# Row order in the two split parts of the normalised rows, and a gather that reads its stationary operand with a stride

## What is computed

```python
h = layer_norm(DN_ALPHA * h + mix @ w_out[l], ln1_g[l], ln1_b[l])
ff = hier_moe(h, w_grp[l], b_grp[l], w_exp[l], b_exp[l], w_gate[l], w_up[l], w_down[l])
ple = (p[l] @ w_ple[l]) * jax.nn.sigmoid(h @ w_ple_gate[l])
h = layer_norm(DN_ALPHA * h + ff + ple, ln2_g[l], ln2_b[l])
# in hier_moe:
hg = jnp.einsum('td,edf->tef', xt, w_gate)
hu = jnp.einsum('td,edf->tef', xt, w_up)
h = jax.nn.silu(hg) * hu * combine[:, :, None].astype(hg.dtype)
return jnp.einsum('tef,efd->td', h, w_down).reshape(B, S, D)
```

## Time and profile before

| | |
|---|---|
| median of 3 runs | 1613.43 us (1612.69 to 1613.9) |
| the profiled execution, its own time | 1613.67 us |
| its span in the profile | 1611.9 us |
| TensorE matmul busy | 1501.9 us (93%) |
| TensorE weight loads busy | 1000.9 us (62%) |
| VectorE, ScalarE, GpSimd busy | 659.7, 494.5, 67.7 us |
| mean granted TensorE clock | 0.984 of full speed |
| DMA | 394.83 MB, 245 GB/s over the span |

### The profile page before, as it was taken

One profiled execution on the slowest core, in us unless ns is written; L12 is line 12 of the kernel. 1 busy time (PEld: TensorE's weight loads), 2 busy tenths in 40 slices (PEclk: granted clock), 3 DMA queues, 4 the chain that ended last, 5 costly groups with the idle time before them and its releaser, 6 DMA issues.

```text
span 1611.9 us, 16579 instructions
## 1 busy us (share of the span) xinstructions
PE 1501.9 (93%) x6640; PEld 1000.9 (62%) x6640; DVE 659.7 (41%) x896; ACT 494.5 (31%) x662; POOL 67.7 (4%) x69
## 2 busy tenths in 40 slices
PE   8999999999999999999999989979988998898872
PEld 6887888887778888888888856423423532342221
DVE  5546665466566554545456544000111021011116
ACT  4444444455544444444444323100200100020011
POOL 0000000046000000000000020000000000000001
PEclk9999999999999999999999998999999999999996
DMA  8654555554434556555659451697999799879991
GB/s 291 190 175 157 181 163 200 163 174 140 153 122 144 182 190 201 183 199 191 195 185 348 165 188 52 278 419 298 373 422 411 299 376 422 350 316 422 422 401 57
DMA packets 130250, 394.83 MB, mean 245 GB/s; under 512 B 11264, under 2 KB 13952, under 8 KB 105600
## 3 DMA queue, kind: packets, MB, share of 16 engines
q1 hardware_dynamic: 121600, 384.45, 64.6%
q10 hardware_dynamic: 8576, 9.36, 1.7%
HBM read 391.69 MB, written 2.10 MB: 244 GB/s over the span
## 4 chain that ended last, share of the span: by engine, by line
PE 80%; DMA 17%; DVE 1%; ACTq 1%; issue 1%; ACT 0%; SPq 0%; POOL 0%; DVEq 0%
PE bank L449 18%; PE bank L450 18%; PE bank L454 17%; DMA moe_ring<-in_w_gate_dram 9%; PE bank L805 7%; PE bank L849 7%; DMA moe_ring<-in_w_down_dram 4%; PE bank L880 4%; DMA moe_ring<-in_w_ple_gate_dram 3%; PE bank L829 2%; PE bank L744 1%; PE bank L779 1%; PE bank L476 1%; PE bank L607 1%; PE bank L629 1%; DMA w_ring<-in_w_in_dram 1%
## 5 line engine op out<-in xcount | busy, mean ns | idle before, releaser
L1411 DVE TENSOR_TENSOR w_lo<-w_ring,w_hi 128x1024 fp32r<-128x1024 f32 (+1 forms) x312 | 381.9, 1226 | 307.4 <-ACT w_hi L1017 306.5
L1017 ACT ACTIVATE w_hi<-w_ring 128x1024 fp32r<-128x1024 f32 (+1 forms) x312 | 327.2, 1050 | 317.0 <-PE bank L454 309.3
L449 PE MATMUL bank<-w_hi,xT_hi 128*128 128x512 f32 (+1 forms) x864 | 347.3, 402 | 2.3 <-ACT w_hi L1017 2.3
L450 PE MATMUL bank<-w_hi,xT_lo 128*128 128x512 f32 (+1 forms) x864 | 335.9, 389 | 0.0
L849 PE MATMUL bank<-moe_ring,xg 128*64 128x512 f32 x1024 | 231.0, 597 | 35.4 <-DMA moe_ring<-in_w_gate_dram 18.2
L454 PE MATMUL bank<-w_lo,xT_hi 128*128 128x512 f32 (+1 forms) x864 | 229.4, 387 | 0.0
L449 PEld LDWEIGHTS bank<-w_hi,xT_hi 128*128 128x128 f32 x864 | 162.7, 188 | 38.8 <-issue 7.1
L849 PEld LDWEIGHTS bank<-moe_ring,xg 128*64 128x64 f32 x1024 | 69.9, 137 | 183.3 <-issue 130.3
L450 PEld LDWEIGHTS bank<-w_hi,xT_lo 128*128 128x128 f32 x864 | 163.0, 189 | 32.6 <-issue 1.9
L454 PEld LDWEIGHTS bank<-w_lo,xT_hi 128*128 128x128 f32 x864 | 161.8, 188 | 33.4
L880 PE MATMUL bank<-moe_ring,moe_hiddenT 128*64 128x512 f32 x448 | 103.3, 606 | 17.2 <-DMA moe_ring<-in_w_down_dram 17.2
(11 more groups left out here) (265 smaller groups left out, 1372.4 us busy)
## 6 DMA issues: line engine op xcount, KB each, us to landing
w_ring<-in_w_in_dram SPq DMA_DIRECT2D x104, 1024.0 KB, 5.0
moe_ring<-in_w_gate_dram SPq DMA_DIRECT2D x32, 2048.0 KB, 15.0
moe_ring<-in_w_up_dram SPq DMA_DIRECT2D x32, 2048.0 KB, 15.6
moe_ring<-in_w_down_dram SPq DMA_DIRECT2D x32, 2048.0 KB, 16.1
w_ring<-in_w_proj_a_dram SPq DMA_DIRECT2D x16, 1024.0 KB, 5.0
w_ring<-in_w_proj_m_dram SPq DMA_DIRECT2D x16, 1024.0 KB, 5.1
w_ring<-in_w_out_dram SPq DMA_DIRECT2D x16, 1024.0 KB, 5.1
moe_ring<-in_w_ple_gate_dram SPq DMA_DIRECT2D x8, 2048.0 KB, 16.8
```

Of the source, the lines that this page charges most:

```text
L449: mm(b, lh(k, m), WH[:, s, kk, 0:width], start=start and kk == 0, stop=False)
L450: mm(b, ll(k, m), WH[:, s, kk, 0:width], start=False, stop=False)
L1017: fn(WH[:, h % 4, :, 0:width], W32[:, h // 2, 2 * (h % 2):2 * (h % 2) + 2, 0:width], ACT.Copy).then_inc(hi_ready, 1)
L1411: v.tensor_tensor(WL[:, h % 4, :, 0:width], W32[:, h // 2, 2 * (h % 2):2 * (h % 2) + 2, 0:width], WH[:, h % 4, :, 0:width].bitcast(F32), A ...
```

## The change

`h1_hi` and `h1_lo` are laid out as [half, 2048] in the order of the rows, as `res` is. ScalarE's copy and VectorE's subtraction are now plain, over 2048 adjacent words. `gather_pair` picks column 16 q + t for q = 0 to 127 out of a row of 2048, so each weight load of the gather reads 128 words that stand 16 words apart, where it read 128 adjacent words. Shapes, types, counts, waits and the order of instructions on every engine are the same. The same function serves the overflow branch, which runs when an expert has more than 64 tokens; the trace has none of its instructions.

```diff
-        h1h = at("h1_hi", [NT, KT, P], Z2, F32R)
-        h1l = at("h1_lo", [NT, KT, P], Z2 + 16384, F32R)
+        h1h = at("h1_hi", [NT, D], Z2, F32R)
+        h1l = at("h1_lo", [NT, D], Z2 + 16384, F32R)
...
                     for part, src in enumerate((h1h, h1l)):
                         for a in range(NT):
-                            last = mm(b[:, kk * TOK:kk * TOK + TOK], src[:, a, 2 * i + kk, :], selg[:, a, :],
+                            last = mm(b[:, kk * TOK:kk * TOK + TOK], src[:, a, 2 * i + kk:D:KT], selg[:, a, :],
                                       start=part == 0 and a == 0, stop=part == 1 and a == 1)
...
             for a in range(NT):
-                fn(h1h[:, a, :, :].rearrange("p t q -> p q t"), RES[:, a, :].rearrange("p (q t) -> p q t", t=KT),
-                   ACT.Copy).then_inc(h1_hi, 1)
+                fn(h1h[:, a, :], RES[:, a, :], ACT.Copy).then_inc(h1_hi, 1)
...
                 dv.wait_ge(h1_hi, a + 1)
-                v.tensor_tensor(h1l[:, a, :, :].rearrange("p t q -> p q t"), RES[:, a, :].rearrange("p (q t) -> p q t", t=KT),
-                                h1h[:, a, :, :].rearrange("p t q -> p q t").bitcast(F32), ALU.subtract).then_inc(h1_lo, 1)
+                v.tensor_tensor(h1l[:, a, :], RES[:, a, :], h1h[:, a, :].bitcast(F32), ALU.subtract).then_inc(h1_lo, 1)
```

## The result

The change makes the kernel slower: 1639.9 us in the median (1638.81 to 1640.6, four runs) against 1613.66 us for the kernel before in the same comparison, a ratio of 1.0162 with a 95% interval of 1.0145 to 1.018. That is 26.2 us. It lies above the range given, and within half a microsecond of the time of the rival that I had given a chance of 0.16. The profiled execution spans 1638.4 us.

A forecast was written before the change was run, and what follows sets the result against it. TensorE's four gathers were taken to bound the end, with DMA engines idle beside them. The sum was 1613.67 + 0 to 1.8 - 0 - 0, forecast 1613.5 us against the median; 8-in-10 range 1611.5 to 1628.5.

The forecast's parts named there:

- What bounds the kernel: All four gathers lie on the path to the end; DMA engines idle beside them, so longer gathers count in full.
- the price: One nanosecond more per matmul of the four gathers, 256 matmuls in all, costs 0.256 us at the end.
- The pace inside a gather: A matmul starts every 120 ns, set by 256 streamed columns; adjacent loads leave the loader 8 to 10 ns slack.
- Part 1: Gather's strided weight loads: they come every 113 ns, under 120, so cost 0, at most 1.8 us.
- The upper bound of 7 ns: Gather's weight loads: if loads limit it, each gets 196 - 189 = 7 ns longer, 1.8 us in all.
- The rule against it: SBUF reads by the gather's loads: each new 16-byte line pays a penalty, so fp32 strides are free only to 4 words.
- Parts 2 and 3: ScalarE's copies save 3.6 us, VectorE's subtractions about 3.1 us; both disappear into waits ended by TensorE, worth 0.
- The halved rate: Gather's strided loads go from 112 to 224 ns each, 26.6 us more, time 1640; chance 0.16.
- Its further fear: In the gathers, less streaming could drop TensorE's clock to the 1.2 GHz level and take the time above 1640.

The follow-up runs named there:

- the split order: The change, strided loads included, with all four gathers split between ring slots: ratio 1.0119 against the kernel before, 1.0143 against the same order with adjacent loads.
- the ladder: Kernel before, the gather's eight pairs loading with strides of 1, 2, 3, 4, 5, 8, 12 and 16 words; one run, 1635.57 us.
- the half-strided kernel: Kernel before with h1_lo in row order and loaded with a stride, h1_hi still adjacent, so half of 256 loads strided: 1628.67 us, ratio 1.0096.

## Why the prediction was wrong, point by point

- **What bounds the kernel.** Right. The gathers were on the path, the price of 0.256 us per nanosecond and matmul held: 103 ns more give 26.4 us, and 26.2 were measured. Half of the loads gave about half. The reason given, that the DMA engines start later by what the gather grows, fits every trace: 93.5 to 94.2 us from the load behind gather 1 or 2 to the next gated product. A load issued sooner was tried at gather 0 alone, where it gained; under the split order 2 us of the longer gather 0 were hidden, so the price holds for the order of work it was read from.
- **The pace inside a gather.** Right. Adjacent words left slack, and the ladder's stride 2 still hides in it.
- **Part 1, the step that failed.** I wrote that I take the cadence of 113 ns of the strided transposes "as the deciding row", and that "an ordinary load is at the slower rate already". Both took a transpose for an ordinary load. The runs show that the plain 4-byte load with a stride of 16 has a cadence of its own, 217 to 225 ns, in fp32r with 64 and 256 columns and in f32 with 128, where I had put 113. That is the term of the sum that failed: 0 to 7 ns per matmul were forecast, and 103 came. The rows had a warning that I noted and explained away: an adjacent transpose lasts 139 ns and an adjacent ordinary load 189, for the same 128 words. If the two take different ways with adjacent words, the pace of one with a stride says nothing about the other. The upper bound of 7 ns drawn from that comparison was worth nothing.
- **The rule against it.** The rule of the 16-byte line (the Trainium skill, "SBUF — State Buffer", Door 1: The DMA port swizzle) was to be trusted more than the nearest row of another kind of operation, though its free stride of 4 words is not what was measured here.
- **Parts 2 and 3.** Right in size and in worth: plain copies of 1.90 and 2.29 us, all of the gain in longer waits, and the ratio of 1.0005 for this half alone.
- **The rivals.** The halved rate, 1640 us, is what happened, at 103 ns more per matmul against the 104 reckoned. Its reason, a second pass over the words, was not seen by any run, so its number is better founded than its mechanism. Its further fear, that the lower clock makes it worse, didn't come true although the clock did fall. The chances were put wrongly: 0.66 rested on one analogy.

## What to carry to other kernels

Before a layout is changed to make copies plain, ask who reads the data afterwards and how often: here two copies behind a wait were made shorter, and 256 weight loads on TensorE's path were made twice as long. For a plain 4-byte stationary operand, beside 256 streamed columns, only strides of 1 and 2 words were free; 3 cost 50 ns and more per matmul, 4 and wider 100 to 150. The cadence of one kind of operation is no bound for another kind when the two differ already where both are measured. And before an order of work is judged by its time, read from SyncE's issues whether any load did start sooner.

## What the runs showed of the hardware

- The strided load's pace does not follow TensorE's clock. In gather 0 of the change the granted clock fell to 0.50, the 1.2 GHz level, for some 3 us, and the count of loads in a microsecond stayed what it was at 1.00 (windows of L829):

```profile
1016.00:1017.00 1.00, 1.00 (x6) 1.00 (x6) 0.50 1.04 442
1024.00:1025.00 1.00, 1.00 (x7) 1.00 (x6) 1.00 0.00 0
```

  The router's adjacent loads, in contrast, went from 32 to 21 in equal windows when the clock fell, and in the half-strided kernel a pair with adjacent loads and 256 columns went from 0.24 to 0.44 us, while a strided pair stayed at 0.43 or 0.44.
- Strides that all touch 128 lines differ: 12 words is the slowest at 265 to 270 ns per matmul, 8 words takes 241, and 16 is the fastest at 220 to 225.
- A transpose pays for a stride of 2 already (208 against 140 ns for its load), where the plain load pays 6 to 8 ns in duration, and in pace 6 ns with 64 columns and nothing with 256; but the transpose's pace stays at 120 ns or less at any stride tried (108 for adjacent words, 120 for 2 and 4, 113 for 16).
